# A float32 transformer on one core: the norm's factor as 128 x 4 columns, its last square summed by TensorE, and renewed x kept in its bank

## The chip, the cores and the metric

One Trainium2 chip, of which the kernel uses one core. The metric is the device time of one execution in microseconds. The time before is 3279.98 us, the median of 3 runs (3278.42 to 3282.66).

## The reference

A batch of one, 512 tokens, width 1024, float32. Four layers run one after the other. Layers 1 and 2 normalize, mix, add, normalize, run a feed-forward with a causal convolution of three taps, and add; their mixers are block attention beside difference attention, then dilated attention beside latent attention. A norm of the residual ends them. Layers 3 and 4 normalize ahead of a block and behind it: `x = x + norm_post(mixer(norm_pre(x)))`, the same with a gated, convolved feed-forward; their mixers merge axial attention, a pooling branch and neighbourhood attention by sigmoid gates. The norm that the change is about:

```
y = xf * lax.rsqrt(jnp.mean(xf * xf, axis=-1, keepdims=True) + EPS)
return y * g
```

The mean is over the 1024 features of one token, so each norm has one factor per token, 512 in all.

## The kernel before, in words

Activations stand transposed: features on the 128 partitions, tokens on 512 columns, eight tiles for 1024 features. `x` is the residual. `hh` and `hl` are its high and low part, times the gain, and weights are split in the same way by GpSimd (L443 to L446: a tiny operation that waits, a cast into `wh`, a subtraction into `wl`). Each product is three matmuls of 512 columns (L464 to L466), so that a projection of eight tiles is 24 matmuls. Projections write the banks PA and PB in turn. The norm's factor is applied behind the projection: `PA * rs`, where `rs` holds the factor of every token on all partitions.

Engines have their own written-out instruction order, and wait for one another by counted semaphores. A program counts them by phase (`counts`, `PHASES1`, `PHASES2`), so that every wait names an absolute count. Phases that the change touches:

- `out0`, `down0`, `out1`, `down1`: the projection back to the residual. For every tile, DVE adds the bank to `x` (`x_add`, L1554) and releases the bank; ACT writes `hh` from `x` (L1008) and squares `x` (L1009); DVE writes `hl` (`remainder`, L1258) and adds the square into `acc` (`add_squares`, L1264). ACT's side is `renew_out`.
- `out2`, `down2` (layers 3 and 4): ACT squares the bank (L1021), DVE copies it to `mix` (L1563), and adds the square into `acc`.
- `norm_final`, `norm_mp`, `norm_fp`: the norm between two stages, with nothing of the next stage to do meanwhile. TensorE's `stat` sums `acc` over the partitions by four matmuls with two columns of ones, so that a token's sum stands on a partition (L505); ACT's `root` takes the root of 128 x 4 (L995, with a table load); DVE's `factor` inverts it (L1237) and multiplies it into the identity, a 128 x 512 diagonal in `acc` (L1238); TensorE's `spread` multiplies it by ones, which puts the factor of every token on all partitions of O0 (L513). DVE then renews `x` (L1285 or L1296 and L1298), ACT writes `hh` and a square, DVE writes `hl`, tile by tile.
- `up2` and `axial_kv` start on these tiles as they come. Behind the projection's step k TensorE sums square k - 1 by a matmul of ones with 512 moving columns into O1 (`sum_square`, L496). Then ACT takes the root of 128 x 512 (`sum_root`, L1004) and DVE the reciprocal of 128 x 512 (`sum_factor`, L1248) into `rs`.
- The pooling stage turns `rs` back into columns by `tokens` (L897), for the values of axial attention. Behind the second pooling tile TensorE waits for the normalized key (`turn_rotate`, L727).
- `moba_v` and `mla_cq` use `stat`, `root`, `factor` and `spread`, with the spread between two parts of the values' projection, and ACT copies O0 to `rs` (L999).

A float32 matmul stands in the trace as two passes, so that a set of four has eight rows.

Of the kernel before, what the change touches and what calls it, by code (L numbers as in the profile page):

```python
# [12 lines left out]
P = 128  # L13
# [47 lines left out]
def counts(kind, seg=None, fin=0, mix=0):  # L61
    c = dict(e=SEGMENTS[seg][0] if seg else 0, a=0, b=0, u=0, g=0, v=0, n=fin, k=0, s=0, q=0, h=0, x=0, z=0,
             m=0, d=fin, r=0, st=0, df=0, pl=0)
    if kind == "x_in":
        c.update(s=1 + DT, q=DT, h=DT)
    elif kind == "v":
        c.update(v=1)
# [8 lines left out]
    elif kind == "mla_cq":  # L76
        c.update(a=1, b=1, d=fin)
# [4 lines left out]
    elif kind == "norm_post":  # L82
        c.update(q=DT, h=DT, x=DT, d=fin + DT)
    elif kind == "norm_final":
        c.update(q=DT, h=DT, x=DT)
    elif kind == "out":
        c.update(a=4, b=4, s=1 + DT, q=DT, h=0 if mix else DT)
    elif kind == "up1":
        c.update(a=FT, b=FT, z=FT, k=1, d=1 + FT * 2)
    elif kind == "up2":  # L90
        c.update(a=FT, b=FT, z=FT, k=1, d=1 + FT * 5)
    elif kind == "merge":
        c.update(a=24, b=24, m=8, d=4 * 2)
    elif kind == "axial_kv":
        c.update(b=3, v=1, k=1, d=2 + TURN_LINKS, r=1)
    elif kind == "pool":
        c.update(a=5, pl=4, d=(1 + 2 + 3 + 4) + 4 * 2)
# [35 lines left out]
    ("up1", counts("up1", "up1")), ("down1", counts("out", "down1")),  # L133
# [55 lines left out]
def build(nc, x_in, weights, consts, cols_in, lam_in, rel_in, rpb_in, strips_rel, strips_na, out):  # L189
    with ExitStack() as ctx:  # L190
# [108 lines left out]
        diag_ready, spread_ready = sem("diag_ready"), sem("spread_ready")  # L299
        sum_ready, root_ready, token_ready = sem("sum_ready"), sem("root_ready"), sem("token_ready")  # L300
# [156 lines left out]
        def _(pe):  # L457
# [16 lines left out]
            def project(dst, s, n, kt=DT, rhs=hs, at=0, w=P, h_from=None, sum_of=None, last_of=None):  # L474

                pe.wait_ge(w_split, n + 3)
                for k in range(kt):
# [5 lines left out]
                    if sum_of is not None and k == SUM_STEP:  # L483
                        sum_acc(sum_of)
                return last
# [14 lines left out]
            def stat(b, spread_now=True):  # L500
# [3 lines left out]
                for t in range(QT):  # L504
                    last = mm(O1[:, 2 * t:2 * t + 2], acc[:, t * P:t * P + P], ones[:, 0:2], start=True, stop=True)  # L505
                last.then_inc(st_ready, 1)
                if spread_now:
                    spread(b)

            def spread(b):  # L510
# [282 lines left out]
            def up(b, squared):  # L793
# [6 lines left out]
                if squared:  # L800
# [11 lines left out]
                    project(PB[:, :], 1, b["e"] + 1).then_inc(entry_done, 1)  # L812
# [80 lines left out]
            def tokens(b):  # L893

                pe.wait_ge(pb_taken, b["b"] + 2)
                for t in range(QT):
                    last = mm(O1[:, 2 * t:2 * t + 2], rs[:, t * P:t * P + P], ident[:, 0:2], start=True, stop=True)  # L897
                last.then_inc(token_ready, 1)

            def pool_tiles(b, kv, ax):  # L900


                def pool_u(g):
                    pe.wait_ge(pa_taken, b["a"] + g + 1)
                    project(PA[:, :], g % 2, b["e"] + g).then_inc(entry_done, 1)

                pool_u(0); k_sum(kv["b"] + 1, kv["r"]); tokens(kv)
# [31 lines left out]
            def moba_stat():  # L939
                pe.wait_ge(table_in, 16 * NTABLE)  # L940
                stat(H("moba_v"), False)
# [14 lines left out]
            stat(b, False)  # L956
# [12 lines left out]
            stat(H("norm_final"))  # L969
            with pe.Fori(0, LAYERS2) as l:  # L970
# [8 lines left out]
                stat(H("norm_mp", l))  # L979
                up(H("up2", l), True); down(H("down2", l))  # L980
                stat(H("norm_fp", l))
# [3 lines left out]
        def _(act):  # L985
# [25 lines left out]
            def renew_out(b, gain_at, e_per=1):  # L1011

                with act.Fori(0, 4) as i:
                    for j, (bank, taken, key) in enumerate(((PA, pa_taken, "a"), (PB, pb_taken, "b"))):
                        if gain_at is None:
                            act.wait_ge(entry_done, b["e"] + e_per * (2 * i + j + 1) + 2)
                        else:
                            act.wait_ge(taken, b[key] + i + 2)
                        act.wait_ge(acc_done, b["s"] + 2 * i + j + 1 - j)
# [915 lines left out]
```

## Time and profile before

| | |
|---|---|
| median of 3 runs | 3279.98 us |
| the profiled execution | 3279.61 us |
| its span | 3277.5 us |
| TensorE busy | 3118.5 us, 95% |
| DVE busy | 1512.5 us, 46% |
| ACT busy | 775.3 us, 24% |
| GpSimd busy | 1654.5 us, 50% |

All durations below are of one profiled execution. TensorE's matmuls are pipelined, and the ends of their rows are modelled: two matmuls in a row overlap in the view. A row "x8" is eight instructions put together, from the first start to the last end. In brackets stands how long the engine had been idle, and what it had waited for.

### The profile page before, as it was taken

The numbers are of one execution on the slowest core, as the hardware profiler recorded it, in microseconds if no ns is written. First come the engines' busy times: TensorE is split into PE (matmuls) and PEld (weight loads), VectorE is DVE, ScalarE is ACT, GpSimd is POOL, SyncE is SP. The second block draws the span as 40 slices with busy tenths as digits, with TensorE's granted clock in tenths as the row PEclk, the third lists the DMA queues.
The fourth block names the chain that finished last, engine by engine and source line by source line (L and its number), as shares of the span: only waits on it lengthen the run. The fifth ranks groups of instructions, "written<-read, shape, count | busy, mean of one in ns | idle before, by whom it ended". The sixth has DMA issues, their size and how long they took to land.

```text
span 3277.5 us, 44864 instructions
## 1 busy us (share of the span) xinstructions
PE 3118.5 (95%) x14402; PEld 2482.7 (76%) x14402; DVE 1512.5 (46%) x2731; ACT 775.3 (24%) x1409; POOL 1654.5 (50%) x1254
## 2 busy tenths in 40 slices
PE   8998999999899999899999989998899999989997
PEld 6776888877678887667788868887667788868885
DVE  4255444333454433633533476632633534576622
ACT  2232221014222211242421122211142421132201
POOL 4334666662166666313246646675313256646674
PEclk9999999999999999889999989999889999989998
DMA  6252223321022233102322222232102222222232
GB/s 158 72 165 66 90 96 106 105 91 58 26 89 97 96 104 107 36 23 57 92 68 96 87 67 98 97 110 84 39 32 62 75 78 96 83 71 96 96 112 74
DMA packets 99597, 274.80 MB, mean 84 GB/s; under 512 B 38126, under 2 KB 38894, under 8 KB 99490
## 3 DMA queue, kind: packets, MB, share of 16 engines
q1 hardware_dynamic: 97328, 269.07, 25.7%
q10 hardware_dynamic: 2162, 4.36, 0.7%
q8 instruction: 60, 0.98, 0.1%
q14 instruction: 47, 0.39, 0.0%
HBM read 269.66 MB, written 11.54 MB: 86 GB/s over the span
## 4 chain that ended last, share of the span: by engine, by line
PE 70%; DVE 4%; issue 2%; ACT 1%; DVEq 0%; ACTq 0%
PE PA L464 11%; PE PA L466 10%; PE PA L465 10%; PE PB L464 8%; PE PB L466 8%; PE PB L465 8%; PE O L598 4%; PE T L592 2%; PE S L561 2%; PE S L653 1%; PE O L496 1%; PE PB L727 0%; DVE hl L1258 0%; DVE tmps L1296 0%; DVE strip L1643 0%
## 5 line engine op out<-in xcount | busy, mean ns | idle before, releaser
L446 POOL TENSOR_TENSOR wl<-raw,wh 128x1024 fp32r<-128x1024 f32 (+2 forms) x416 | 1122.5, 2698 | 33.4
L443 POOL TENSOR_TENSOR zero<-zero 128x1 f32<-128x1 f32 x416 | 82.3, 198 | 1554.7 <-PE PA L466 817.6
L464 PE MATMUL PA<-hh,wh 128*128 128x512 f32 x1392 | 566.5, 407 | 28.2 <-DVE hl L1258 10.7
L466 PE MATMUL PA<-hh,wl 128*128 128x512 f32 x1392 | 549.5, 395 | 0.0
L465 PE MATMUL PA<-hl,wh 128*128 128x512 f32 x1392 | 549.3, 395 | 0.0
L444 POOL CAST wh<-raw 128x1024 fp32r<-128x1024 f32 (+2 forms) x416 | 475.6, 1143 | 0.0
L464 PEld LDWEIGHTS PA<-hh,wh 128*128 128x128 f32 x1392 | 265.9, 191 | 130.7 <-issue 60.8
L464 PE MATMUL PB<-hh,wh 128*128 128x512 f32 x896 | 357.7, 399 | 0.9 <-DVE yl L1467 0.9
L466 PE MATMUL PB<-hh,wl 128*128 128x512 f32 x896 | 350.3, 391 | 0.0
L465 PE MATMUL PB<-hl,wh 128*128 128x512 f32 x896 | 349.9, 391 | 0.0
L466 PEld LDWEIGHTS PA<-hh,wl 128*128 128x128 f32 x1392 | 265.6, 191 | 57.1
L465 PEld LDWEIGHTS PA<-hl,wh 128*128 128x128 f32 x1392 | 266.4, 191 | 54.8 <-issue 3.0
L1042 ACT ACTIVATE probs<-biased,stats 128x512 f32<-128x512 f32 (+2 forms) x240 | 155.2, 647 | 453.2 <-PE T L592 267.7
L1572 DVE SCALAR_TENSOR_TENSOR tmps<-S,cols,tmps 128x511 f32<-128x511 f32 (+1 forms) x264 | 197.9, 750 | 39.7 <-DVE tmps L1572 20.0
L464 PEld LDWEIGHTS PB<-hh,wh 128*128 128x128 f32 x896 | 168.8, 188 | 44.4 <-issue 10.7
L466 PEld LDWEIGHTS PB<-hh,wl 128*128 128x128 f32 x896 | 168.9, 188 | 36.0
L465 PEld LDWEIGHTS PB<-hl,wh 128*128 128x128 f32 x896 | 168.9, 189 | 34.0 <-issue 1.2
L598 PE MATMUL O<-V,probsT 128*128 128x64 f32 (+1 forms) x1072 | 145.2, 273 | 11.8 <-ACT probsT L1048 10.8
L592 PEld LDWEIGHTS T<-ident,probs 128*128 128x128 f32 x792 | 99.5, 148 | 68.2 <-issue 39.1
L598 PEld LDWEIGHTS O<-V,probsT 128*128 128x128 f32 x1072 | 135.0, 193 | 19.1 <-ACT probsT L1048 17.0
L1258 DVE SCALAR_TENSOR_TENSOR hl<-x,cols,hh 128x512 fp32r<-128x512 f32 (+1 forms) x80 | 129.1, 1620 | 39.1 <-ACT hh L1008 38.8
L1130 ACT ACTIVATE T<-tmps 128x512 f32<-128x512 f32 x88 | 53.0, 602 | 395.4 <-DVE tmps L1572 395.4
(278 smaller groups left out, 5035.5 us busy)
## 6 DMA issues: line engine op xcount, KB each, us to landing
raw<-in_w_up SPq DMA_DIRECT2D x176, 512.0 KB, 3.4
raw<-in_w_down SPq DMA_DIRECT2D x64, 768.0 KB, 4.2
raw<-in_w_merge SPq DMA_DIRECT2D x48, 768.0 KB, 4.2
raw<-in_w_out SPq DMA_DIRECT2D x32, 512.0 KB, 3.4
strips_na<-in_rpb SPq DMA_DIRECT2D x1, 7620.0 KB, 32.1
raw<-in_w_pool SPq DMA_DIRECT2D x12, 512.0 KB, 3.4
raw<-in_w_na_qk SPq DMA_DIRECT2D x12, 512.0 KB, 3.4
raw<-in_w_na_v SPq DMA_DIRECT2D x8, 512.0 KB, 3.5
```

The costliest lines, as they stand in the source:

```text
L443: nc.gpsimd.tensor_tensor(zero[:, :], zero[:, :], zero[:, :], ALU.add)
L444: nc.gpsimd.tensor_copy(wh[s][:, 0:width], raw[s][:, 0:width]).then_inc(w_head, 1)
L446: nc.gpsimd.tensor_tensor(wl[s][:, 0:width], raw[s][:, 0:width], wh[s][:, 0:width].bitcast(F), ALU.subtract).then_inc(w_split, 1)
L464: mm(dst, h_, rh, start=first, stop=False)
L465: mm(dst, h_, rl, start=False, stop=False)
L466: return mm(dst, l_, rh, start=False, stop=last)
L561: mm(SB[t % 2][:, 0:L], q_sb[r, qt * P:qt * P + P], k_sb[r, 0:L], start=True, stop=True).then_inc(s_ready, 1)
L592: last = nc.tensor.transpose(TB[t % 2][:, k * P:k * P + P], probs[t % 2][:, k * P:k * P + P], ident[:, :])
L598: last = mm(OB[t % 2][:, 0:dv], probsT[t % 2][:, k * P:k * P + P], values(k), start=(k == 0), stop=(k == L // P - 1))
L1042: A(probs[t % 2][:, 0:L], biased[t % 2][:, 0:L], ACT.Exp, scale=-1.0, bias=mn[:, t % 8:t % 8 + 1], accum_out=den[:, t % 8:t % 8 + 1]).then ...
L1258: STT(out=tile(hl, j), in0=tile(x, j), scalar=cols[:, bass.ds(gain_at + j, 1)], in1=tile(hh, j).bitcast(F), op0=ALU.mult, op1=ALU.subtract ...
L1572: ins = STT(out=dst[:, lo:hi], in0=src[:, lo - d:hi - d], scalar=w(k), in1=dst[:, lo:hi], op0=ALU.mult, op1=ALU.add)
```

## The change

`factor` no longer builds the diagonal: it only inverts the 128 x 4 columns (`rsT`). `spread` makes four matmuls whose stationary operand is one column of `rsT` read 128 times, with the identity as moving operand. `stat_last` takes the place of `stat` in the five norms: token sums of `acc` (which now holds seven squares), then those of the last square in `tmp[1]`, in one accumulation, then the spread. `sum_square` sums each square by the same four two-column matmuls in place of the 512-column one, and `up2` and `axial_kv` then go through `root`, `factor` and `spread`, with the spread placed behind step 2 of the next projection. `tokens` and its copy go, as `rsT` is there. In `out0`, `down0` and `out1` DVE writes the renewed tile into the bank; ACT and DVE split it from there, and ACT copies it to `x` at the end and only then releases the bank. `down1`, whose norm renews x anyway, no longer splits it. The counters and the dependency chain of DVE are adapted.

```diff
-            def sum_square(b, j):
-                pe.wait_ge(sq_ready, b["q"] - DT + j + 1)
-                last = mm(O1[:, :], ones[:, :], squares[:, j, :], start=(j == 0), stop=(j == DT - 1))
-                if j == DT - 1:
-                    last.then_inc(sum_ready, 1)
+            def token_sums(src, first, last):
+                for t in range(QT):
+                    out_ = mm(O1[:, 2 * t:2 * t + 2], src[:, t * P:t * P + P], ones[:, 0:2], start=first and t == 0,
+                              stop=last and t == QT - 1)
+                if last:
+                    out_.then_inc(st_ready, 1)
+            def sum_square(b, j):
+                pe.wait_ge(sq_ready, b["q"] - DT + j + 1)
+                token_sums(squares[:, j, :], j == 0, j == DT - 1)
+            def stat_last(b):
+                pe.wait_ge(acc_done, b["s"])
+                pe.wait_ge(o_taken, b["u"] + 2)
+                token_sums(acc, True, False)
+                pe.wait_ge(sq_ready, b["q"])
+                token_sums(tmp[1], False, True)
+                spread(b)
             def spread(b):
-                pe.wait_ge(diag_ready, b["n"] + 1)
-                mm(O0[:, :], ones[:, :], acc[:, :], start=True, stop=True).then_inc(spread_ready, 1)
+                pe.wait_ge(inv_ready, b["n"] + 1)
+                for t in range(QT):
+                    last = mm(O0[:, t * P:t * P + P], rsT[:, t:t + 1].to_broadcast([P, P]), ident[:, :], start=True, stop=True)
+                last.then_inc(spread_ready, 1)
...
                     pe.wait_ge(pb_taken, b["b"] + 1)
-                    project(PB[:, :], 1, b["e"] + 1).then_inc(entry_done, 1)
+                    project(PB[:, :], 1, b["e"] + 1, after=(None, None, lambda: spread(b))).then_inc(entry_done, 1)
...
-                pool_u(0); k_sum(kv["b"] + 1, kv["r"]); tokens(kv)
+                pool_u(0, (None, None, lambda: spread(kv))); k_sum(kv["b"] + 1, kv["r"])
...
+            def renew_out(b, gain_at):
+                with act.Fori(0, 4) as i:
+                    for j, (bank, taken) in enumerate(((PA, pa_taken), (PB, pb_taken))):
+                        n = 2 * i + j
+                        act.wait_ge(xs_ready, b["xs"] + n + 1)
+                        A(tile(hh, n), bank[:, :], ACT.Copy, scale=cols[:, bass.ds(gain_at + n, 1)]).then_inc(hh_ready, 1)
+                        act.wait_ge(h_ready, b["h"] + n + 1)
+                        act.wait_ge(acc_done, b["s"] + 2 * i + 1)
+                        A(tmp[j][:, :], bank[:, :], ACT.Square).then_inc(sq_ready, 1)
+                        A(tile(x, n), bank[:, :], ACT.Copy).then_inc(taken, 1)
...
             def factor(b):
-                chain_at(b["d"])
                 dve.wait_ge(std_ready, b["n"] + 1)
-                link(v.reciprocal(rsT, rsT))
-                TT(acc[:, :].rearrange("p (t n) -> p t n", t=QT),
-                   ident[:, :].rearrange("p (a n) -> p a n", a=1).to_broadcast([P, QT, P]),
-                   rsT.rearrange("p (t a) -> p t a", a=1).to_broadcast([P, QT, P]), ALU.mult).then_inc(diag_ready, 1)
+                v.reciprocal(rsT, rsT).then_inc(inv_ready, 1)
...
                 clear(b)
                 with dve.Fori(0, 4) as i:
+                    for j, bank in enumerate((PA, PB)):
+                        n = 2 * i + j
+                        dve.wait_ge(entry_done, b["e"] + e_per * (n + 1) + 2)
+                        TT(bank[:, :], tile(x, n), bank[:, :], ALU.add).then_inc(xs_ready, 1)
+                        dve.wait_ge(hh_ready, b["h"] + n + 1)
+                        STT(out=tile(hl, n), in0=bank[:, :], scalar=cols[:, bass.ds(gain_at + n, 1)],
+                            in1=tile(hh, n).bitcast(F), op0=ALU.mult, op1=ALU.subtract).then_inc(h_ready, 1)
+                        add_squares(b, n, tmp[j][:, :])
...
-            up(H("up1"), CAT["conv1"], False); x_add(H("down1"), 2, CAT["final"])
+            up(H("up1"), CAT["conv1"], False); x_sum(H("down1"), 2)
```

## Rows read from the trace of the kernel before

**Rows 1.** The page, TensorE's line: busy time, share of the span, instructions.

```profile
PE 3118.5 (95%) x14402; PEld 2482.7 (76%) x14402; DVE 1512.5 (46%) x2731; ACT 775.3 (24%) x1409; POOL 1654.5 (50%) x1254
```

**Rows 2.** TensorE's waits: what waited, for what, total us, times, longest us.

```profile
PE O L505 <- DVE acc L1264: 19.8, 5, 4.9
...
PE PA L464 <- DVE hl L1258: 10.7, 6, 3.8
...
PE PB L727 <- DVE tmps L1479: 8.7, 2, 4.4
```

**Rows 3.** Timeline of the first `norm_mp`: start us, us, engine, line, operation.

```profile
1892.77 0.60 ACT L1021 ACTIVATE tmps<-PB 128x512 f32<-128x512 f32 x1 [4.69 <-PE PB L466]
...
1893.38 1.28 ACT L995 ACT_TABLE_LOAD   x1
...
1894.06 2.34 POOL L446 TENSOR_TENSOR wl<-raw,wh 128x1024 fp32r<-128x1024 f32 x1
1894.13 2.82 DVE L1264 TENSOR_TENSOR acc<-acc,tmps 128x512 f32<-128x512 f32 x1
...
1897.00 1.86 PE L505 MATMUL O<-ones,acc 128*128 128x2 f32 x8 [4.27 <-DVE acc L1264]
1898.90 0.26 ACT L995 ACTIVATE stats<-O,eps 128x4 f32<-128x4 f32 x1 [4.24 <-PE O L505]
1899.20 0.18 DVE L1237 RECIPROCAL stats<-stats 128x4 f32<-128x4 f32 x1 [2.25 <-ACT stats L995]
1899.41 0.69 DVE L1238 TENSOR_TENSOR acc<-ident,stats 128x512 f32<-128x512 f32 x1
...
1900.16 2.08 PE L513 MATMUL O<-acc,ones 128*128 128x512 f32 x2 [1.29 <-DVE acc L1238]
1902.41 0.75 DVE L1296 SCALAR_TENSOR_TENSOR tmps<-mix,cols,O 128x512 f32<-128x512 f32 x1 [2.31 <-PE O L513]
```

**Rows 4.** Timeline of `norm_final`: the last `hh`, the spread, the first renewal.

```profile
1304.52 0.72 ACT L1008 ACTIVATE hh<-x,cols  x1 [13.64 <-DVE x L1554]
...
1311.48 2.08 PE L513 MATMUL O<-acc,ones 128*128 128x512 f32 x2 [1.29 <-DVE acc L1238]
1313.59 1.40 DVE L1285 SCALAR_TENSOR_TENSOR x<-x,cols,O 128x512 f32<-128x512 f32 x2 [2.17 <-PE O L513]
```

**Rows 5.** Timeline of the last `norm_fp`: square, token sums, spread.

```profile
3252.55 0.60 ACT L1021 ACTIVATE tmps<-PB 128x512 f32<-128x512 f32 x1 [14.21 <-PE PB L466]
...
3254.65 1.05 PE L505 MATMUL O<-ones,acc 128*128 128x2 f32 x8 [2.14 <-DVE acc L1264]
...
3257.00 1.92 PE L513 MATMUL O<-acc,ones 128*128 128x512 f32 x2 [1.29 <-DVE acc L1238]
```

**Rows 6.** TensorE's timeline: sums and small matmuls within the stream, three places.

```profile
38.24 0.95 PE L505 MATMUL O<-ones,acc 128*128 128x2 f32 x8
39.05 0.49 PE L537 MATMUL S<-wh,hh 128*128 128x512 f32 x1
...
229.68 0.61 PE L598 MATMUL O<-V,probsT 128*128 128x128 f32 x4
...
1341.89 1.88 PE L496 MATMUL O<-squares,ones 128*128 128x512 f32 x4
1343.20 0.79 PE L464 MATMUL PA<-hh,wh 128*128 128x512 f32 x1
```

**Rows 7.** DVE's timeline in `out1`: one tile and the next one's addition.

```profile
911.34 0.69 DVE L1554 TENSOR_TENSOR x<-x,PA 128x512 f32 x1 [0.72 <-PE PA L466]
913.24 2.22 DVE L1258 SCALAR_TENSOR_TENSOR hl<-x,cols,hh  x1 [1.21 <-ACT hh L1008]
915.38 0.68 DVE L1264 TENSOR_TENSOR acc<-acc,tmps 128x512 f32<-128x512 f32 x1
916.78 0.69 DVE L1554 TENSOR_TENSOR x<-x,PB 128x512 f32 x1 [0.72 <-PE PB L466]
```

**Rows 8.** Windows, start of `axial_kv`: stretch, us, busy by engine, clock, DMA share.

```profile
1316.00:1325.00 9.00, 8.98 (x33) 7.89 (x33) 8.56 (x13) 8.10 (x14) 0.00 (x0) 0.50 0.01 2
```

More of the change, by code:

```diff
@@ L132 @@
     ("out1", counts("out", "out1")),
-    ("up1", counts("up1", "up1")), ("down1", counts("out", "down1")),
+    ("up1", counts("up1", "up1")), ("down1", counts("out", "down1", mix=1)),
     ("norm_final", counts("norm_final", fin=1)),
@@ L484, in project @@
                         sum_acc(sum_of)
+                    if k < len(after) and after[k] is not None:
+                        after[k]()
                 return last
@@ L891, in axial_kv, with pool_u @@
                 sum_square(b, DT - 1)
[L893 to L898, printed above, removed]
             def pool_tiles(b, kv, ax):
-                def pool_u(g):
+                def pool_u(g, after=()):
                     pe.wait_ge(pa_taken, b["a"] + g + 1)
-                    project(PA[:, :], g % 2, b["e"] + g).then_inc(entry_done, 1)
-                pool_u(0); k_sum(kv["b"] + 1, kv["r"]); tokens(kv)
+                    project(PA[:, :], g % 2, b["e"] + g, after=after).then_inc(entry_done, 1)
+                pool_u(0, (None, None, lambda: spread(kv))); k_sum(kv["b"] + 1, kv["r"])
                 pool_u(1); turn_rotate(kv["b"] + 1, kv["r"], tmp[2])
@@ L1185, in _ @@
             renew_out(H("out1"), CAT["ffn_norm1"])
-            sum_root(H("up1")); up(H("up1"), ACT.Gelu); renew_out(H("down1"), CAT["final"])
+            sum_root(H("up1")); up(H("up1"), ACT.Gelu); square_out(H("down1"), 2, True)
             b = H("norm_final")
@@ L1510, in axial_values @@
             def axial_values(b):
-                dve.wait_ge(token_ready, b["l"] + 1)
-                link(v.tensor_copy(rsT, O1[:, 0:8].rearrange("p (t two) -> p t two", two=2)[:, :, 0]))
                 for t, bank in enumerate((S0, S1, T0, T1)):
@@ new lines, in x_sum, with both @@
+            def x_sum(b, e_per):
+                clear(b)
+                def both(i, adds):
+                    for j, (bank, taken) in enumerate(((PA, pa_taken), (PB, pb_taken))):
+                        n = 2 * i + j
+                        dve.wait_ge(entry_done, b["e"] + e_per * (n + 1) + 2)
+                        TT(tile(x, n), tile(x, n), bank[:, :], ALU.add).then_inc(taken, 1)
+                        if j < adds:
+                            add_squares(b, n, tmp[j][:, :])
+                with dve.Fori(0, 3) as i:
+                    both(i, 2)
+                both(3, 1)
@@ L1558, in mix_copy, with both @@
             def mix_copy(b):
                 clear(b)
-                with dve.Fori(0, 4) as i:
+                def both(i, adds):
                     for j, (bank, taken) in enumerate(((PA, pa_taken), (PB, pb_taken))):
-                        dve.wait_ge(sq_ready, b["q"] + 2 * i + j + 1)
-                        v.tensor_copy(tile(mix, 2 * i + j), bank[:, :]).then_inc(taken, 1)
-                        add_squares(b, 2 * i + j, tmp[j][:, :])
+                        n = 2 * i + j
+                        dve.wait_ge(sq_ready, b["q"] + n + 1)
+                        v.tensor_copy(tile(mix, n), bank[:, :]).then_inc(taken, 1)
+                        if j < adds:
+                            add_squares(b, n, tmp[j][:, :])
@@ L1566, in conv @@
+                with dve.Fori(0, 3) as i:
+                    both(i, 2)
+                both(3, 1)
             def conv(dst, src, col, taps, last):
```

91 lines of the change are left out of this document (44 added, 47 removed).

## The prediction

> **What bounds the kernel now.** The page comes first: TensorE has work in 95% of the span [rows 1], and most of the chain of waits is projection matmuls. Nothing of DVE or ACT counts unless TensorE stands still for it, so the next view is TensorE's waits [rows 2]. The reader is to see there that it waits 19.8 us for the last addition into `acc` ahead of the norm's token sums (L505), 10.7 us for renewed `hl`, and 8.7 us, twice 4.4, for the key's turn. The first lies in the five norms that stand between stages: `norm_final`, and per layer `norm_mp` and `norm_fp`. There all engines work one after the other.
>
> The timeline of one of them [rows 3] gives the steps. ACT squares the last bank (1892.77 to 1893.37), and DVE, having copied it, adds the square into `acc` from 1894.13. That addition takes 2.82 us, and its end, 1896.95, lies after the end of GpSimd's subtraction (1894.06 to 1896.40): it stood behind it, since the same operation takes 0.68 us at 915.38 with no subtraction beside it [rows 7]. Then eight token-sum passes at the 1.2 GHz level (1.86), root (0.26), reciprocal (0.18), diagonal (0.69), and the spread, after which DVE begins to renew x at 1902.41. From the start of the square to there it is 9.64 us. Three norms are like this, within 0.1 us (both `norm_mp` and the first `norm_fp`); one stands. In the last norm GpSimd has finished: 3252.55 to 3257.00, a spread of 1.92 and 0.15 to DVE, 6.52 us [rows 5].
>
> **Part 1: the last square goes to TensorE, the diagonal goes.** After the change TensorE runs the sums of `acc` while ACT squares; `acc` then holds seven squares, the last of them of a tile that ended one projection (5.44 us) before. A set of eight token-sum passes at full clock costs, from the stream: L505 at 38.24, the matmul behind it ends at 39.54, 0.39 of that is its own, so 0.91 us [rows 6]. Sums of `acc` therefore run to about 1893.65 (TensorE's last matmul ends as the square starts, 1892.7), those of the square to 1894.6. ACT's table load ends at 1894.66, and that is now late: root 1894.70 to 1894.96, reciprocal to 1895.18 with the gaps of today (0.04 each), spread from 1895.25. Today it starts at 1900.16: 4.91 us earlier.
>
> The four spread matmuls are eight passes of 128 columns with eight weight loads. The nearest row is L598 with 128 columns, four passes in 0.61 us [rows 6]: 1.22 for eight, at full clock, and 0.17 until DVE starts as now. Today it is 2.25 us from L513 to L1296, at half clock. The trace shows no weight load from one column read 128 times. From below it costs what L598's does. From above I take twice the load's share. A token-sum pass is nearly all load (0.91 / 8 = 0.11), so eight times 0.11 more, 0.9 us a spread. I take the lower end, since source and bytes are no larger for the array. Level of the clock: in this pause TensorE fell to 1.2 GHz before L505 (its eight passes 1.86 after a wait of 4.27), but in the last norm they still ran in 1.05 us, at 2.4 GHz, after a wait of 2.14 [rows 5]. After the change the pause before the spread is only some 0.7 us. At 2.4 GHz the start of DVE comes at 1895.25 + 1.39 = 1896.64 (gain 5.77 us); at 1.2 GHz, 1.22 us later (gain 4.55).
>
> `norm_final` [rows 4]: the square no longer stands behind `hh`, so it starts at 1304.52 and ends at 1305.13; sums to 1306.1; table load 1305.15 to 1306.43; root, reciprocal, spread from 1307.0 instead of 1311.48 (4.48), and 2.11 becomes 1.39: 5.20 us. The last `norm_fp` [rows 5]: the spread starts 2.48 us after the square's start as above, 3255.03 instead of 3257.00 (1.97), and 1.92 + 0.15 becomes 1.39: 2.65 us.
>
> Sum at full clock: 3 × 5.77 + 5.20 + 2.65 = 25.2 us. What follows in these places begins with DVE's renewal, whose pace does not change, so TensorE's first matmul moves by as much. A norm's saving is not eaten by the next wait: renewal starts at about 1896.64, just behind the subtraction's end at 1896.40.
>
> The Trainium skill, SBUF — State Buffer, section "Who interferes with whom", says that a `tensor_tensor` with both inputs in SBUF contends with GpSimd's reads, and that the loser waits to the end; the 2.82 us above agree. By that rule a renewal that began 0.3 us earlier would be held at its first addition of two SBUF inputs, for tenths of a us; the sum would stay within 1 us.
>
> **Part 2: new work in TensorE's stream.** `up2` and `axial_kv` (two each) summed the squares by 512-column matmuls of ones. Two of them take: L496 at 1341.89, the next matmul ends at 1343.99, less 0.39, 1.71 for two, 0.86 each [rows 6]. Token sums cost 0.91. That is 0.05 × 32 = 1.6 us, of which I take 1.0, for in `up2` TensorE waits for renewed `hl` between them [rows 2]. Bound: the last norm's set took 1.05 us [rows 5], so 0.19 × 32 = 6.1; below, zero. Then each of the four gets a spread, 1.22 us, after step 2 of the next projection. The wait in front of it costs nothing: root, reciprocal and hops are 0.26 + 0.18 + 0.15, and nine matmuls of a projection of 24 in 5.44 us (2.0) cover them; without cover it would be 0.6 each, and all of TensorE's queue stands behind it. The root and the reciprocal of 512 columns go, but TensorE did not wait for them here, so this is worth nothing. `tokens` goes from the pooling stage (a set of 0.9 us), but TensorE then stands 4.4 us for the key's turn [rows 2], so its removal is worth nothing either: what counts there is DVE's chain, which starts with the first pooling tile, 1.22 later, and loses the copy of `rsT` (about 0.2, by L1237, as small). So 2 × 1.22 + 2 × 1.02 = 4.5 us.
>
> `moba_v` and `mla_cq` spread inside the values' projection: 1.22 instead of 0.86, 2 × 0.36 = 0.7 us.
>
> **Part 3: renewed x in its bank.** In `out0`, `down0`, `out1` tiles come every 5.44 us (911.34 to 916.78) [rows 7], in `down0`, with 22 steps, more slowly. The chain from the bank's end: add 0.69 (as L1554, also one SBUF and one PSUM input), `hh` 0.72 [rows 4], `hl` 0.75 (as L1296, one input in a bank [rows 3]) where today it is 2.22 behind GpSimd, square 0.6, copy to x 0.6, with hops of 0.1 to 0.3 each: some 4.1 us. The bank is free 1.3 us before TensorE needs it again (5.44 later). TensorE does not wait for `hl` there today either. Cost and gain 0; if the two-input forms reading a bank did stand behind GpSimd, the chain would be the 1.5 us longer that `hl` is today, 5.6, and TensorE would wait 0.2 us a tile. `down1` drops `hh` and `hl`, on no path.
>
> **Sum.** 25.2 - 1.0 - 4.5 - 0.7 = 19.0 us, all five spreads of the norms at 2.4 GHz. All at 1.2 GHz: 19.0 - 5 × 1.22 = 12.9. I take two of five at the lower level, because the level fell at some of today's pauses and not at others: 19.0 - 2.4 = 16.6. The profiled execution took 3279.61 us, 2.1 beyond its span of 3277.5, and the median is 3279.98, 0.4 more. From the median: 3279.98 - 16.6 = 3263.4, say 3263. The likeliest case's own range is 3258 to 3268.
>
> **Rivals.**
> Clock kept. Granted clock is 0.50 from 1316 to 1325 [rows 8], where `axial_kv` begins after the norm's pause. If the shorter pauses leave the clock at 2.4 GHz, half of these 9 us comes back, and as much at the first `norm_fp`; `up2` runs at DVE's pace and gets none. 2 × 4.5 more, and the two spreads: 3263.4 - 9.0 - 2.4 = 3252 at the most; 3254 is taken. Against it: before the first renewed tile TensorE still has nothing for up to 3.8 us [rows 2], and it fell in a pause of 4.3 [rows 3]. The Trainium skill, TensorE: Matmul & The Clock Gate, section "Part 1: The HAM clock gate", says that activity releases the throttle and idling restores it at instants that the kernel doesn't choose, so both levels stay open.
>
> Gain mostly eaten. The repeated column's load costs the upper bound (11 spreads × 0.9 = 9.9), or token sums 5 us more with the clock low. For it: no row shows this load. Then 16.6 - 9.9 = 6.7 left, 3273, down to no change.
>
> The bank is the new wait (other side, slower). From L1554's end TensorE gets its bank only after four more operations on two engines in turn. TensorE waits from a chain of 5.44 us; `out0` and `out1` hold 16 such turns (six tiles each, and the first two banks of the projection behind), `down0` none at its pace. If both DVE operations on the bank are held the full 1.5 us by GpSimd, the chain is 4.1 + 3.0 = 7.1 us and costs 1.66 × 16 = 26.6 us: 3263.4 + 26.6 = 3290. The gain is gone from a chain of 6.5 (1.04 × 16 = 16.6). Against it: L1554 takes 0.69 beside GpSimd.
>
> The last square's sum does not hide. If TensorE's `acc` sums only ran after the square, 0.9 × 5 = 4.5 us less: 3268, in the likeliest case's range.
>
> **How the numbers follow.** Forecast 0.62 (with the last rival), clock kept 0.14, gain eaten 0.16, bank 0.08. The measurement tells 0.2%, 6.6 us, from no change: faster means under 3273.4. All of the first two are faster, 0.07 of the third, none of the fourth (0.05 of it slower, 0.03 the same): faster 0.83, same 0.12, slower 0.05. The range 3253 to 3273 takes in most of clock kept and of the eaten gain, and leaves out the bank's and the rest.
>
> **What would show it.** In each norm: L505's passes twice, the second set behind ACT's square; root behind the table load; no 512-column DVE operation between root and spread; from square to renewal 3.9 us instead of 9.6 (2.48 to the spread). In the stream: 0.9 per set of eight, four spreads of 1.2, no wait ahead of them; the key's turn 1 us later relative to its stage. In `out0` and `out1`: TensorE without waits, `hl` at 0.75. I am wrong if TensorE waits on ACT's copy to x, if a pass of the spread takes over 0.2 us at full clock, or if the renewal stands behind GpSimd.

## The result and the profile after

| | before | after |
|---|---|---|
| time, median (lowest to highest) | 3281.32 us (3278.42 to 3283.51, 4 runs) | 3314.60 us (3313.95 to 3315.04, 4 runs) |
| span of the profiled execution | 3277.5 us | 3312.4 us |
| mean granted TensorE clock | 0.970 | 0.955 |
| TensorE busy | 3118.5 us (95%) | 3178.9 us (96%) |

The ratio after to before is 1.0098, 95% interval 1.0084 to 1.0112: slower by about 1%. (The ratios in this document are those of the record; they are not exactly the quotients of the medians printed beside them.) The forecast was 3263 us, within 3253 to 3273, and faster. Both numbers are off, and so is the sign.

The page of the changed kernel opens with this busy time and these slices (each digit of PEclk is the granted clock of a fortieth of the span, in tenths):

```profile
PE 3178.9 (96%) x14692; PEld 2564.8 (77%) x14692; DVE 1433.1 (43%) x2709; ACT 784.2 (24%) x1429; POOL 1658.8 (50%) x1254
...
PEclk9999999999999999789999979998789999979998
```

TensorE is busy for 60.4 us more than before, more than the span grew, so its waits have become shorter and its work longer. The waits say that what was predicted for the norms did happen (TensorE's waits of the changed kernel: engine, tile, line and releaser, then us in total, times, longest):

```profile
PE PA L464 <- DVE hl L1271: 10.5, 5, 3.7
...
PE PB L742 <- DVE tmps L1493: 8.7, 2, 4.4
...
PE O L527 <- DVE stats L1253: 3.7, 5, 0.7
```

The line of 19.8 us [rows 2] is no longer there; what is left ahead of the norms' spreads is 3.7 us. The norm itself is next: the timeline of `norm_mp` after the change, which answers to [rows 3].

```profile
1907.09 0.95 PE L498 MATMUL O<-ones,acc 128*128 128x2 f32 x8
1907.28 0.60 ACT L1040 ACTIVATE tmps<-PB 128x512 f32<-128x512 f32 x1 [4.69 <-PE PB L466]
...
1907.90 1.28 ACT L1003 ACT_TABLE_LOAD   x1
1907.91 0.69 DVE L1595 COPY mix<-PB 128x512 f32<-128x512 f32 x1 [1.83 <-ACT tmps L1040]
...
1907.93 1.05 PE L498 MATMUL O<-ones,tmps 128*128 128x2 f32 x8
1908.58 2.35 POOL L446 TENSOR_TENSOR wl<-raw,wh 128x1024 fp32r<-128x1024 f32 x1
1909.19 0.26 ACT L1003 ACTIVATE stats<-O,eps 128x4 f32<-128x4 f32 x1
1909.49 0.18 DVE L1253 RECIPROCAL stats<-stats 128x4 f32<-128x4 f32 x1 [0.89 <-ACT stats L1003]
...
1909.72 1.43 PE L527 MATMUL O<-ident,stats 128*128 128x128 f32 x8 [0.73 <-DVE stats L1253]
...
1911.31 0.75 DVE L1310 SCALAR_TENSOR_TENSOR tmps<-mix,cols,O 128x512 f32<-128x512 f32 x1 [1.65 <-PE O L527]
```

From the start of the square (1907.28) to DVE's renewal (1911.31) it is 4.03 us; it was 9.64. The sum of `acc` runs beside the square, the second set at 1907.93 stands close behind it, and DVE does no 512-column work between root and spread. `norm_final` follows the forecast too. From the end of the projection before it to its first renewed matmul it was 12.57 us (1303.45 to 1316.02) and is 6.95 (1304.77 to 1311.72): 5.62 less, for a forecast of 5.20. The rows of the changed kernel that answer to [rows 4]:

```profile
1304.61 0.95 PE L498 MATMUL O<-ones,acc 128*128 128x2 f32 x8
1306.31 1.05 PE L498 MATMUL O<-ones,tmps 128*128 128x2 f32 x8 [0.76 <-ACT tmps L1040]
1308.10 1.16 PE L527 MATMUL O<-ident,stats 128*128 128x128 f32 x8 [0.73 <-DVE stats L1253]
1311.72 0.47 PE L898 MATMUL S<-wh,hh 128*128 128x128 f32 x1 [2.46 <-DVE hl L1271]
```

What is lost comes behind the norm. First the changed kernel's timeline of one step of `axial_kv`:

```profile
1318.17 0.73 PE L464 MATMUL PB<-hh,wh 128*128 128x512 f32 x1
1318.71 0.63 PE L465 MATMUL PB<-hl,wh 128*128 128x512 f32 x1
...
1319.56 1.70 PE L498 MATMUL O<-ones,squares 128*128 128x2 f32 x8
1321.12 0.45 PE L898 MATMUL S<-wh,hh 128*128 128x128 f32 x1
1321.37 0.41 PE L899 MATMUL S<-wl,hh 128*128 128x128 f32 x1
```

and the same kind of step in the kernel before:

```profile
1326.58 0.28 PE L885 MATMUL T<-wh,hl 128*128 128x128 f32 x1
1326.69 0.45 PE L464 MATMUL PB<-hh,wh 128*128 128x512 f32 x1
1326.98 0.39 PE L465 MATMUL PB<-hl,wh 128*128 128x512 f32 x1
...
1327.43 1.02 PE L496 MATMUL O<-squares,ones 128*128 128x512 f32 x2
```

Every matmul, the unchanged ones too, takes longer (0.63 for 0.39 with 512 columns, 0.41 for 0.28 with 128), and the set of eight token-sum passes takes 1.70 where I had 0.91. The windows tell why (stretch, its length, busy us of PE, PEld, DVE, ACT and POOL with the instructions, granted clock, DMA share, GB/s). After:

```profile
1312.00:1356.00 44.00, 44.00 (x184) 41.68 (x183) 8.26 (x13) 7.79 (x13) 6.32 (x6) 0.50 0.04 12
```

and before, with the level that [rows 8] showed only for the first 9 us:

```profile
1325.00:1343.00 18.00, 18.00 (x104) 13.93 (x104) 0.00 (x0) 0.00 (x0) 4.41 (x5) 0.99 0.09 30
```

The granted clock is 0.50 (1.2 GHz) for 44 us on end, with TensorE busy in all of them; before, it was back at 2.4 GHz after some 9 us. The groups of the changed kernel by form (count, shortest, median and longest ns, first and last start) say that this holds in most of the sets:

```profile
L498 PE MATMUL O<-ones,squares x256: 207/352/353, 1319.6 to 2932.6; 128*128 128x2 f32 x128
L498 PE MATMUL O<-ones,acc x56: 165/251/251, 39.0 to 3290.8; 128*128 128x2 f32 x56
```

The median pass over the squares takes 352 ns (passes overlap), that of the same form over `acc`, in the norms, 251.

Two lengths measure it, and they are used for all experiments. **Keys** is from the first matmul of `axial_kv` to the key's turn: 1316.02 to 1361.27 before (45.25 us), 1311.72 to 1375.94 after (64.22), 18.97 more. **FFN** (the feed-forward stage) is from the first renewed matmul of `up2` to the first of its second pair of projections: 1905.99 to 1927.91 before (21.92), 1914.89 to 1948.38 after (33.49), 11.57 more. The second layer repeats both (45.82 and 64.13; 21.93 and 33.51). That is 18.97 + 18.31 + 11.57 + 11.58 = 60.4 us lost; the span grew by 34.9 (3277.5 to 3312.4), so all else together gained 25.5.

### The profile page after: what moved, and what is told of

Same layout as the page of the kernel before. It is cut to its first block, busy times and chain, and to the rows that moved or that the text cites. A ratio compares the mean times of both kernels' runs of the same rounds, so it can differ in the third digit from the quotient of the medians.

```text
span 3312.4 us, 45411 instructions
## 1 busy us (share of the span) xinstructions
PE 3178.9 (96%) x14692; PEld 2564.8 (77%) x14692; DVE 1433.1 (43%) x2709; ACT 784.2 (24%) x1429; POOL 1658.8 (50%) x1254
## 3 DMA queue, kind: packets, MB, share of 16 engines
q1 hardware_dynamic: 97328, 269.07, 25.2%
## 4 chain that ended last, share of the span: by engine, by line
PE 72%; DVE 3%; issue 2%; ACT 1%; DVEq 0%; ACTq 0%
PE PA L464 11%; PE PA L466 10%; PE PA L465 10%; PE PB L464 8%; PE PB L466 8%; PE PB L465 8%; PE O L613 4%; PE T L607 2%; PE S L576 2%; PE O L498 1%; PE S L668 1%; PE PB L742 0%; PE O L527 0%; DVE strip L1687 0%; ACT probsT L1065 0%
## 5 line engine op out<-in xcount | busy, mean ns | idle before, releaser
L464 PE MATMUL PA<-acth,wh 128*128 128x512 f32 x352 | 137.4, 390 | 0.0
```

Source lines behind the costliest of these rows:

```text
L464: mm(dst, h_, rh, start=first, stop=False)
```

## The experiments

Every kernel is the changed one with the edit shown (the last two start from the one with 512-column sums), and its ratio is against the kernel before on the same chip. The chips differ a little (the kernel before has medians from 3281.3 to 3284.0), so differences of a few us between rows measured on different chips say little. All kernels, in the order of the text:

| kernel | time, us | ratio (95% interval) | keys | FFN |
|---|---|---|---|---|
| before | 3281 to 3284 | 1 | 45.25 | 21.92 |
| changed | 3314.6 | 1.0098 (1.0084 to 1.0112) | 64.22 | 33.49 |
| 512-column sums again | 3255.4 | 0.9916 (0.9899 to 0.9932) | 48.07 | 21.92 |
| 128 columns a pass | 3258.3 | 0.9922 (0.9898 to 0.9946) | 45.01 | 22.88 |
| 64 columns | 3295.7 | 1.0053 (1.0032 to 1.0075) | 64.23 | 22.88 |
| 32 columns | 3315.9 | 1.0103 (1.0085 to 1.0121) | 64.36 | 33.54 |
| filler behind each set | 3334.5 | 1.0153 (1.0133 to 1.0173) | 76.60 | 31.82 |
| sums in the next projection | 3323.2 | 1.0125 (1.0102 to 1.0148) | 65.51 | 34.46 |
| 128 columns in `axial_kv` alone | 3281.5 | 1.0000 (0.9990 to 1.0010) | 45.13 | 32.71 |
| 128 columns in `up2` alone | 3294.5 | 1.0028 (1.0017 to 1.0040) | 64.41 | 22.85 |
| 128 columns in sets 0 to 3 | 3264.1 | 0.9933 (0.9912 to 0.9953) | 45.11 | 26.07 |
| filler, all sets behind it | 3303.0 | 1.0058 (1.0040 to 1.0076) | 57.59 | 33.83 |
| 512-column sums, no bank | 3253.7 | 0.9916 (0.9898 to 0.9933) | 48.07 | 21.93 |
| 512-column sums, last square on DVE | 3265.5 | 0.9949 (0.9932 to 0.9966) | 45.90 | 21.92 |

**The sums of the squares undone.** With them come back the root and the reciprocal of 512 columns and `tokens`, and the spread in the stream goes. My theory: the narrow token sums in the stream keep TensorE at 1.2 GHz, and all of the loss is theirs. Rivals: the passes and spreads cost more than I had priced, or the loss is in the norms or the bank.

```
-                token_sums(squares[:, j, :], j == 0, j == DT - 1)
+                last = mm(O1[:, :], ones[:, :], squares[:, j, :], start=(j == 0), stop=(j == DT - 1))
...
-                root(bk)
+                sum_root(bk)
...
+            def tokens(b):   # as in the kernel before
```

> Part 2 undone alone: up2 and axial_kv sum the squares by the 512-column matmuls again, with root and reciprocal of 512 columns; norms, bank and the two value spreads stay changed. Theory (clock): the two-column sums between the projections' matmuls keep TensorE at 1.2 GHz through these four stages (granted clock 0.50 over 44 us in the changed kernel, where before it rose after 9). So the 61 us that the four stages lost come back and the norms' gain stays: about 3256 us, and the granted clock rises within 13 us of the first renewed tile. Rival (the passes themselves): token sums and spreads cost more than I priced, at either clock; undoing them gives back 32 x 0.8 + 4 x 1.2 = 30 us, about 3284. Rival (the norms' saving is not real, or the bank costs): at or above 3281.

Measured: 3255.4 us, 28.6 under the kernel before beside it (3284.0). This part alone turned a gain of 0.8% into a loss of 1.0%. A window within `axial_kv`, in this kernel:

```profile
1330.00:1340.00 10.00, 10.00 (x63) 8.13 (x63) 0.00 (x0) 0.00 (x0) 2.67 (x2) 1.00 0.17 54
```

**The width of a pass.** The same eight passes a set, with the same weight loads, but 128 columns of ones instead of 2 (`root` reads column 0 of each group). It tells the clock from the cost of the passes: wider passes can only cost more by themselves.

```
-                    out_ = mm(O1[:, 2 * t:2 * t + 2], src[:, t * P:t * P + P], ones[:, 0:2], start=first and t == 0,
+                    out_ = mm(O1[:, w * t:w * t + w], src[:, t * P:t * P + P], ones[:, 0:w], start=first and t == 0,
```

> One size changed: the sums of the squares in up2 and axial_kv take 128 moving columns of ones in place of 2 (the root reads every 128th column); the same loads, the same order. Theory (clock): columns streamed in these stages are again those of before, the clock rises: 3256 + 16 x 0.25 + 4 spreads of 1.2 = about 3266. Rival (the passes themselves): 8 passes with 128 columns cost 1.1 to 2.2 us instead of 0.9 to 1.7: 3314.6 + 32 x 0.2 to 0.5, 3321 to 3330.

> The same size at 32 columns. Theory (clock): it shows where between 2 and 128 the stage's clock turns; if the level is still held at 1.2 GHz about 3315 to 3318, if not about 3262, and if some of the four stages turn and others don't, between. Rival (the passes themselves): at most 1 us from the changed kernel, 3315, with the same clock.

> The size between: 64 moving columns per token-sum pass in up2 and axial_kv. At 32 the granted clock stayed at 0.50 over the stage (3316), at 128 it rose (3258). Theory (clock): one of these two times or, with some stages turned, one between, and the granted clock of each stage says which; no other term is over 3 us. Rival (time falls smoothly with the size, for a reason other than the clock's level): about 3290 with the clock as at 32.

Measured: 3258.3 with 128, 3315.9 with 32, and 3295.7 with 64, where the FFN is that of 128 columns and the keys are those of 2. Wider passes, which are more work, make the kernel 56.3 us faster (58 by the ratios). The same window of the kernel with 128 columns:

```profile
1330.00:1340.00 10.00, 10.00 (x75) 9.34 (x75) 0.18 (x1) 0.26 (x1) 3.56 (x3) 1.00 0.06 23
```

and of the one with 64:

```profile
1330.00:1340.00 10.00, 10.00 (x43) 9.42 (x43) 0.00 (x0) 0.00 (x0) 3.52 (x3) 0.50 0.16 54
```

**Filler.** If more columns help, a wide matmul behind each narrow set should help as well. It goes into the unused columns of the bank and nothing reads it.

```
                 token_sums(squares[:, j, :], j == 0, j == DT - 1)
+                if j < DT - 1:
+                    mm(O1[:, 8:S], ones[:, :], squares[:, j, 8:S], start=False, stop=False)
```

> The changed kernel with work added: behind each two-column sum of a square (but the last) a matmul of ones with 504 moving columns, whose output nobody reads. Theory (clock): though 28 matmuls of two passes are added, the clock rises again in the four stages, and the time falls: 3256 + 28 x 0.9 + 4 spreads of 1.2 = about 3286, some 28 us under the changed kernel's 3314.6. Rival (the passes themselves): nothing gets faster, the added work comes on top: 3314.6 + 28 x 0.85 = 3338 or more.

Measured: 3334.5. I had expected 3286; the time that came is near the rival's 3338. The same window of this kernel has 0.50 all the same:

```profile
1330.00:1340.00 10.00, 10.00 (x34) 7.70 (x34) 0.00 (x0) 0.00 (x0) 3.51 (x3) 0.50 0.01 2
```

In `axial_kv`, then, wide work in the stream isn't enough while the narrow set stands beside it. In the FFN it was enough. There the level rises in the third narrow set and stays, with the sets and the filler going on:

```profile
1945.55 1.18 PE L498 MATMUL O<-ones,squares 128*128 128x2 f32 x8
...
1948.21 0.95 PE L498 MATMUL O<-ones,squares 128*128 128x2 f32 x8
```

The FFN length falls from 33.49 to 31.82, though it has seven wide matmuls more. So the rival's time came near without its reason: the keys pay for the filler at 1.2 GHz (12.4 us more a stage), the FFN gets 1.7 us back. As a whole this was a miss, and the last of the experiments on the clock takes it up again.

**The sums in the next projection.** All eight sets, two at a time, behind steps 0 to 3 of the projection that follows, and the spread behind its step 6.

```
-                        if k > 0:
-                            sum_square(b, k - 1)
-                    sum_square(b, DT - 1)
...
-                    project(PB[:, :], 1, b["e"] + 1, after=(None, None, lambda: spread(b))).then_inc(entry_done, 1)
+                    project(PB[:, :], 1, b["e"] + 1, after=late(b)).then_inc(entry_done, 1)
```

> The changed kernel with its two-column sums moved out of the first projection of up2 and axial_kv: two sets behind each of the steps 0 to 3 of the next projection, the spread behind step 6. The number of passes stays. Theory (clock held low by what stands between the matmuls after the norm's pause): the first projection now runs without them and TensorE rises to 2.4 GHz in axial_kv before the sums come; 16 x 0.9 us of sums in up2 are no longer beside DVE's pace: 3256 + 5 + 10 = about 3271. Rival (wherever sets of small passes stand, the clock falls to 1.2 GHz for that stretch): each of four stages loses some 5 us more, about 3290. Rival (the passes' number costs it): no change from 3314.6.

Measured: 3323.2, a second miss. The timeline shows two things that I had not thought of:

```profile
1333.40 0.73 PE L464 MATMUL PB<-hh,wh 128*128 128x512 f32 x1
...
1337.24 0.73 PE L464 MATMUL PB<-hh,wh 128*128 128x512 f32 x1
...
1345.43 0.48 PE L464 MATMUL PA<-hh,wh 128*128 128x512 f32 x1
...
1346.21 2.59 PE L498 MATMUL O<-ones,squares 128*128 128x2 f32 x16
...
1350.09 3.41 PE L498 MATMUL O<-ones,squares 128*128 128x2 f32 x16
```

The steps of `axial_kv` now have no sums between them at all, and still come every 3.84 us with matmuls of 0.73. Their own twelve matmuls of 128 columns and three of 512 leave the level low (it was 0.50 from 1311.6 to 1343.6, with TensorE busy throughout), so the 512-column sum before was what brought the clock up there. And where the clock had risen in the next projection (0.48 at 1345.43), the pairs of sets took it down again: 16 passes in 2.59, then in 3.41 us, twice 1.70. In the FFN two pairs take 1.84 each, the third 2.68, the fourth 3.41.

**Which stage.** 128 columns in `axial_kv` alone, then in `up2` alone (2 columns in the other).

```
+            def sum_square(b, j, wide=True):
...
+                token_sums(squares[:, j, :], j == 0, j == DT - 1, P if wide and j < 8 else 2, P if wide else 2)
```

> The sums of squares get 128 moving columns a pass in axial_kv alone, and keep 2 in up2. Theory (each stage's clock hangs on its own sums): axial_kv runs as with 128 columns everywhere (mostly 1.00 from 1330 us), up2 stays as in the changed kernel, so of the 56.3 us between the changed kernel (3314.6) and 128 columns everywhere (3258.3) the part of up2, 2 x 11.6 = 23 us by the stretches, stays lost: 3281 us, 3276 to 3287. Rival (the stages are not independent, one level carries over into the next): the gain is all there or all gone, 3258 or 3315 us.

> The opposite half: 128 moving columns a pass in up2 alone, 2 in axial_kv. Theory: up2 is quick and axial_kv stays at 1.2 GHz, 2 x 19 = 38 us lost against 128 columns everywhere (3258.3): 3296 us, 3290 to 3301; with the run above it should add up, so that the two losses are together near 56 us. Rival: 3258 or 3315 us.

Measured: 3281.5 and 3294.5. Over 128 columns everywhere they lose 23.2 and 36.2 us, together 59.4, against 56.3 for both at once and 60.4 by the two lengths. Each stage's loss is its own.

**Raised, then narrow.** Sets 0 to 3 with 128 columns, sets 4 to 7 with 2.

```
+                token_sums(squares[:, j, :], j == 0, j == DT - 1, P if wide and j < 4 else 2, P if wide else 2)
```

> Sets 0 to 3 of each stage with 128 moving columns a pass, sets 4 to 7 with 2. If the narrow passes only keep a low clock low, and do not lower a high one, the clock rises behind the first sets and stays up: 3255 to 3262 us. If narrow passes also lower a high clock (as the late sums of the fifth run made it look), the granted clock falls again in the second half of the stage or never rises in axial_kv: 3280 us or more, with 0.50 again in axial_kv behind 1335 us. I expect the second, 3287 us.

Measured: 3264.1, where I had leaned to 3287: a miss, on the side of the first theory. In `axial_kv` the level comes up in the wide sets and stays up in the narrow ones (the last wide set and the first two narrow ones of this kernel's timeline):

```profile
1333.15 1.05 PE L498 MATMUL O<-ones,squares 128*128 128x128 f32 x8
...
1336.08 0.95 PE L498 MATMUL O<-ones,squares 128*128 128x2 f32 x8
...
1339.01 0.95 PE L498 MATMUL O<-ones,squares 128*128 128x2 f32 x8
```

0.95 a set, close to the 0.91 of the forecast: at that level my price was right. In the FFN it doesn't stay up. The length is 26.07 there, 3.2 more than with 128 columns throughout, and the two narrow sets in a row at its end run at the low level:

```profile
1917.16 0.95 PE L498 MATMUL O<-ones,squares 128*128 128x2 f32 x8
...
1918.88 3.41 PE L498 MATMUL O<-ones,squares 128*128 128x2 f32 x16
```

The granted clock is 1.00 from 1912.0 to 1918.6 and 0.50 from 1918.6 to 1925.4, so it fell ahead of that pair, behind two single narrow sets with waits of 0.2 to 0.3 us for DVE about them. With 128 columns throughout, the level stayed up there. The second layer's FFN repeats the fall (27.66). So half of the theory that I had leaned to is right in this stage: narrow sets can lower a high clock.

**Filler again, the narrow sets apart.** The 512-column matmul behind each step as in the kernel before, but for the last (seven of them, overwritten later), and the 64 narrow passes in one bunch behind the eighth step.

```
+            def fill(b, j):
+                pe.wait_ge(sq_ready, b["q"] - DT + j + 1)
+                mm(O1[:, :], ones[:, :], squares[:, j, :], start=(j == 0), stop=(j == DT - 2))
...
-                            sum_square(b, k - 1)
-                    sum_square(b, DT - 1)
+                            fill(b, k - 1)
+                    for j in range(DT):
+                        sum_square(b, j)
```

> Behind each step stands the 512-column matmul of the kernel before (its result is overwritten, so it is filler), and all eight sets of narrow passes stand in one bunch behind the last step. The stream of the eight steps is then that of the kernel with 512-column sums (3255.4). If the granted clock hangs on what runs between the steps, it rises there as before, and the bunch costs 8 x 0.91 = 7.3 us a stage at the full clock, four stages 29 us: 3284 us. If the bunch lowers the clock itself, it costs 8 x 1.7 = 13.6 us and the stage behind it starts at 1.2 GHz: 3310 us or more. If the narrow passes have nothing to do with it (so the filler of the second run would not have helped for another reason), the clock in axial_kv stays at 0.50 over the whole stage: 3345 us.

Measured: 3303.0, between the first case (3284) and the second (3310). The timeline has both halves:

```profile
1337.62 1.02 PE L510 MATMUL O<-squares,ones 128*128 128x512 f32 x2
1338.47 11.20 PE L498 MATMUL O<-ones,squares 128*128 128x2 f32 x64
1349.53 0.77 PE L464 MATMUL PA<-hh,wh 128*128 128x512 f32 x1
1350.10 0.63 PE L465 MATMUL PA<-hl,wh 128*128 128x512 f32 x1
```

The filler alone does raise the clock. Its windows, ahead of the bunch and over it:

```profile
1330.00:1340.00 10.00, 10.00 (x66) 8.17 (x64) 0.00 (x0) 0.00 (x0) 2.06 (x3) 1.00 0.15 52
1340.00:1350.00 10.00, 10.00 (x52) 10.00 (x53) 0.00 (x0) 0.26 (x1) 1.45 (x1) 0.56 0.17 52
```

The bunch takes 11.20 us, more than 8 × 0.91 and less than 8 × 1.70, and the projection behind it starts at the 1.2 GHz level: the narrow passes lowered a clock that was high. The other three bunches take 9.98, 10.09 and 10.16 us. That makes 41.4 us in all, and by the ratios this kernel is 1.42% (46.6 us) behind the one with the 512-column sums.

**The bank undone**, from the kernel with 512-column sums: DVE adds into x and frees the bank, and `hh`, `hl` and the square are made from x.

```
-                        TT(bank[:, :], tile(x, n), bank[:, :], ALU.add).then_inc(xs_ready, 1)
+                        xt = tile(x, n)
+                        TT(xt, xt, bank[:, :], ALU.add).then_inc(taken, 1)
+                        remainder(b, n, gain_at)
```

> e1_wide_sums with part 3 undone too: DVE adds the bank to x and releases it, ACT and DVE split from x. Prediction's pricing: bank 0, so the same time as e1_wide_sums, 3255, within 1.5 us. Rival (the bank's holding costs or gains what the clock hid): more than 3 us to either side.

Measured: 3253.7, the same ratio (0.9916) as with it. Within the intervals, which are some 6 us to either side, the bank is worth nothing either way.

**The last square back on DVE**, from the same kernel: DVE adds the eighth square into `acc`, and TensorE sums once. The diagonal stays out.

```
-                token_sums(acc, True, False)
-                pe.wait_ge(sq_ready, b["q"])
-                token_sums(tmp[1], False, True)
+                token_sums(acc, True, True)
...
-                both(3, 1)
+                both(3, 2)
```

> e1_wide_sums with the last square of the five norms added into acc by DVE again, then summed; the diagonal stays out. By the rows of before: in the three norms with GpSimd's subtraction the sums start 2.4 to 3.6 us later and at 1.2 GHz, so the spread starts 4.2 us later than in e1 and takes up to 1.2 more; norm_final some 3 to 4, the last 1.3. Theory (the norms' gain is mostly the addition behind GpSimd): 3 x 4.7 + 4 + 1.3 = 19 us over e1_wide_sums, about 3274. Rival (the diagonal and its wait were the larger part): within 8 us of e1, 3263 at most.

Measured: 3265.5, 10.1 us behind the kernel with 512-column sums, not the 19 that I had expected, and not within the rival's 8. In this kernel the last addition of `norm_mp` is not held by GpSimd (timeline):

```profile
1895.62 0.68 DVE L1284 TENSOR_TENSOR acc<-acc,tmps 128x512 f32<-128x512 f32 x1
1895.68 2.83 POOL L446 TENSOR_TENSOR wl<-raw,wh 128x1024 fp32r<-128x1024 f32 x1
...
1901.03 0.75 DVE L1317 SCALAR_TENSOR_TENSOR tmps<-mix,cols,O 128x512 f32<-128x512 f32 x1 [2.29 <-PE O L527]
```

0.68 us where it took 2.82 before [rows 3]. It starts 0.06 us ahead of GpSimd's subtraction, and the subtraction is the one that takes longer (2.83 for 2.34). The addition ahead of it is held as before (2.85 us from 1890.34), and nobody waits for that one. From ACT's square (1894.38) to the renewal it is 6.65 us, against 4.67 (1887.97 to 1892.64) with the last square on TensorE: 1.98 us. The norms differ: it is 1.98 and 1.97 in the two `norm_mp`, 1.17 and 1.16 in the two `norm_fp`, and 4.09 in `norm_final`, where the last addition is held now and was not in the kernel before (0.68 us at 1307.59 there):

```profile
1306.23 2.69 DVE L1284 TENSOR_TENSOR acc<-acc,tmps 128x512 f32<-128x512 f32 x1 [0.80 <-ACT tmps L1047]
```

Together that is some 10 us.

## Why the prediction was wrong

**The step that failed** is in Part 2: "Token sums cost 0.91", set against 0.86 for the 512-column sum, a loss of 1.0 us with a bound of 6.1. I took the price of a set from rows at 2.4 GHz and let the stream around it keep its speed. Most sets cost 1.70, and with them in place of the 512-column sums every other matmul between them ran at 1.2 GHz: 60.4 us in four stages, where 5.5 were forecast for the sums and spreads there. Both the same passes with 128 columns and the old 512-column sums bring the time to 3258.3 and 3255.4. What I had not asked is what raised the clock in these stages: [rows 8] showed 0.50 where `axial_kv` began, and the stretch behind it had 0.99, so something in the stream had brought it up. By the experiments it was, in `axial_kv`, the 512-column sums, and the change took them out. I had the clock as a rival in one direction only ("clock kept"), and in the rival "gain mostly eaten" I gave "token sums 5 us more with the clock low" for something that costs twelve times that.

The Trainium skill, TensorE: Matmul & The Clock Gate, section "Part 1: The HAM clock gate (the "warmup" mystery)", says that the gate is set by how busy the array has been, and this is how I used it. The trace does not agree if the profile's busy count is taken for that: busy 44.00 of 44 us, level 0.50. The measurement decides.

**Part 1, right.** From square to renewal 3.87 us was worked out (1892.77 to 1896.64) and 4.03 measured, with the spread at 1.43 instead of 1.22. In `norm_final` it was 1.16. A load of the repeated column takes 192 ns in the median, as one of `acc` does, so the lower end was the right one. From the last projection's end to the first renewed matmul the four norms ahead of a stage are 5.62, 5.62, 6.18 and 5.62 us shorter, and the last norm is 1.95 from square to renewal: 25.0 in all, for 25.2 at the full clock or 22.8 with two spreads at the low level. Two were (1.98 us each, both in `norm_fp`), and two more were partly (1.43 and 1.42). The root stood behind the table load as said (1909.18, 1909.19). With the old sums back, what is left of the change should give 25.2 less 0.7 for the spreads of the values, 24.5 us. It gives 22.4 by the spans of the profiled executions (3277.5 to 3255.1) and 28.6 by the medians of one chip, on either side of that. In that profile four of the five spreads ran at the 1.2 GHz level (2.07 to 2.08 us), and the first keys length is 2.8 us more than before (48.07). The last square on TensorE is some 10 of it.

**Part 2's other terms, not contradicted at the full clock.** With 128 columns a pass the kernel is 3.0 us above the one with 512-column sums, for a forecast of 1.0 + 4.5 = 5.5 for the narrow ones; the intervals of the two are too wide to tell these apart. The FFN takes 22.88 against 21.92, 0.96 more, near the spread of 1.22. TensorE waits 4.4 us for the key's turn as before; no wait appears ahead of the spreads in the stream (the 3.7 us in L527 are the norms' five).

**Part 3, right**: cost and gain 0, 3253.7 against 3255.4 with the same ratio. In `out1` of the changed kernel `hl` takes 0.75 us with one input in a bank, as priced, though GpSimd's subtraction runs beside it (913.80 to 916.20):

```profile
914.34 0.75 DVE L1568 SCALAR_TENSOR_TENSOR hl<-PA,cols,hh 128x512 f32 x1 [1.03 <-ACT hh L1025]
```

From the addition's start to the end of the copy to x it is 3.67 us (912.61 to 916.28), for 4.1 forecast. One sign that I had named for being wrong did appear: TensorE waits for ACT's copy to x once, 3.3 us, behind the first bank of `out0`. It cost 0.3 us at most, since at the same place it waited 3.0 us for GpSimd's split before.

**The rivals.** With 128 columns a pass, and so with the clock up in these stages, the kernel came to 3258, inside my range. That it is so near my 3263 is in part luck: the kernel before took 3284.0 beside it, not the 3280.0 that I had started from, and the gain is 25.6 us, where I had forecast 16.6. "The bank is the new wait" was given as the only slower case (3290, chance 0.08), and it didn't happen; slower had a chance of 0.05 in all. No case held what did happen.

**What stays open.** What the chip counts when it sets the level is not known from these runs. They show that in `axial_kv` a narrow set between the steps kept a low clock low even with a wide matmul beside it, while in the FFN the same filler brought the clock up. Single narrow sets, one per step, didn't lower a high clock in `axial_kv`, but in the FFN it fell behind two of them. Several pairs in the next projection, and a bunch of 64 passes, were followed by a fall. Why 64 columns, or the filler, raised the clock in the FFN but not in `axial_kv` is only argued: the latter's own matmuls are mostly of 128 columns, and they did not raise it alone.

## What to carry to other kernels

Before you replace a wide matmul in a dense stream by narrow ones, read the granted clock of the stage and ask which work brought it up: busy time doesn't show it, the stretch that follows a pause does. If a narrow product is all that is needed, try the same passes with more columns as well, since they can be cheaper than the narrow ones. Price an operation at both levels of the clock, and with it everything that runs between its repetitions.

## What the runs showed of the hardware

- TensorE busy in every us of 44 ran at 1.2 GHz throughout, with sets of eight passes of 2 columns between matmuls of 128 and 512 columns. With 128 columns in those passes, the granted clock was 1.00 from 1330 to 1340 us.
- Narrow passes lowered a high level: 64 of them in 11.20 us, with matmuls of 0.63 behind them where 0.39 stood ahead.
- A wide matmul of filler beside each narrow set left the level at 0.50 in a stream of mostly 128-column matmuls (1330 to 1340 us). With the same filler in a stream of 512-column ones the level rose (sets of 1.70 us, then of 0.95 from 1948.21 on).
- A weight load from one column read 128 times costs no more than another: 192 ns in the median for both, and four spread matmuls in 1.16 us at the full clock, for 1.22 by the nearest row.
- Which addition GpSimd holds (2.82 us for 0.68) moves with the schedule. In the kernel before, the last one was held in `norm_mp` and not in `norm_final`; with the last square back on DVE it is the other way round. An addition that started 0.06 us ahead of the subtraction took 0.68, and the subtraction 2.83.
